# A smaller ring for GpSimd's dynamic DMAs and a seventh gate/up weight buffer in its place

## The reference, cut to what matters

```python
x = x + m @ w_out
f = hier_moe(rmsnorm(x, ln2_g).reshape(B * T, D), w_rg, b_rg, w_re, b_re, wg, wu, wd)
return x + f.reshape(B, T, D)
...
for g in range(N_GROUPS):
    hg = jnp.einsum('td,edf->tef', x, wg[g])
    hu = jnp.einsum('td,edf->tef', x, wu[g])
    hh = jax.nn.silu(hg) * hu * comb[:, g, :, None]
    y = y + jnp.einsum('tef,efd->td', hh, wd[g])
```

## Time and profile before

| what | value |
|---|---|
| median of 3 runs | 772.43 us |
| lowest, highest | 770.75, 772.51 us |
| the profiled execution: span from first to last instruction | 779.7 us |
| PE busy | 716.8 us (92%) |
| DVE, ACT, POOL busy | 397.7, 212.9, 194.6 us |
| HBM read, written | 154.27, 25.78 MB |
| mean granted TensorE clock | 0.952 |

### The profile page before, as it was taken

One profiled execution on the slowest core, in us unless ns is written; L12 is line 12 of the kernel. 1 busy time (PEld: TensorE's weight loads), 2 busy tenths in 40 slices (PEclk: granted clock), 3 DMA queues, 4 the chain that ended last, 5 costly groups with the idle time before them and its releaser, 6 DMA issues.

```text
span 779.7 us, 11121 instructions
## 1 busy us (share of the span) xinstructions
PE 716.8 (92%) x4071; PEld 349.9 (45%) x4071; DVE 397.7 (51%) x1107; ACT 212.9 (27%) x502; POOL 194.6 (25%) x208
## 2 busy tenths in 40 slices
PE   9999999899999999999999769999999999789293
PEld 6555556566666655455555532233232332222040
DVE  0776677754875854765655732333223332211275
ACT  3565646412452463112211201011110111000032
POOL 1011111010230333111112136544455444300111
PEclk9999999999999999899999869999999999779787
DMA  8911030030110016772221968699999999999794
GB/s 317 339 55 42 28 124 1 28 142 1 61 61 0 1 54 253 256 282 106 84 109 66 387 224 306 235 357 358 345 413 425 422 427 424 424 427 424 309 388 198
DMA packets 35544, 173.56 MB, mean 223 GB/s; under 512 B 6882, under 2 KB 13486, under 8 KB 25226
## 3 DMA queue, kind: packets, MB, share of 16 engines
q1 hardware_dynamic: 27058, 154.27, 50.5%
q0 software_dynamic: 8000, 17.24, 5.9%
q10 hardware_dynamic: 432, 1.34, 0.4%
HBM read 154.27 MB, written 25.78 MB: 231 GB/s over the span
## 4 chain that ended last, share of the span: by engine, by line
PE 65%; DVE 13%; DMA 9%; ACT 5%; issue 5%; SPq 1%; POOL 1%; DVEq 0%; POOLq 0%; ACTq 0%
PE PS L2185 17%; PE PS L2201 9%; PE PS L2004 6%; PE PS L1996 6%; PE PS L1982 4%; PE PS L1832 4%; DMA BIG<-in_wexp 4%; PE PS L1963 3%; PE PS L1833 2%; PE PS L1952 2%; DVE RD L1220 2%; DMA RD<-xtab,rot 2%; DMA BIG<-ypair 2%; PE PS L1816 2%; PE PS L2044 1%
## 5 line engine op out<-in xcount | busy, mean ns | idle before, releaser
L2185 PE MATMUL PS<-BIG,RD 128*32 128x512 f32 x1408 | 166.7, 620 | 13.3 <-issue 10.3
L2185 PEld LDWEIGHTS PS<-BIG,RD 128*32 128x32 f32 x1408 | 46.0, 114 | 118.3 <-issue 118.3
L876 POOL DMA_INDIRECT RD<-xtab,rot x84 | 85.0, 1012 | 35.5 <-issue 24.4
L2201 PE MATMUL PS<-BIG,RD 128*32 128x512 f32 x616 | 79.7, 592 | 2.0 <-DMA BIG<-in_wexp 0.9
L1684 DVE SCALAR_TENSOR_TENSOR RD<-RD,PS 128x256 f32<-128x256 f32 x22 | 9.2, 418 | 141.7 <-ACT RD L1140 141.7
L1832 PE MATMUL PS<-BIG 128*128 128x512 f32 x128 | 66.1, 598 | 0.3 <-DMA BIG<-in_wqkv 0.3
L773 POOL TENSOR_TENSOR stat<-stat,mhalf 128x1 f32<-128x1 f32 (+1 forms) x27 | 15.5, 575 | 188.9 <-DVE stat L1210 84.0
L1140 ACT ACTIVATE RD<-PS 128x256 f32<-128x256 f32 x22 | 8.4, 383 | 192.5 <-PE PS L2185 145.3
L2004 PE MATMUL PS<-BIG 128*128 128x512 f32 x128 | 60.5, 617 | 0.0
L1996 PE MATMUL PS<-BIG 128*128 128x512 f32 x128 | 59.2, 607 | 0.0
L1982 PE MATMUL PS<-BIG 128*128 128x344 f32 x192 | 57.3, 454 | 0.0
(11 more groups left out here) (321 smaller groups left out, 1017.9 us busy)
## 6 DMA issues: line engine op xcount, KB each, us to landing
BIG<-in_wexp SPq DMA_DIRECT2D x30, 2048.0 KB
BIG<-in_wexp SPq DMA_DIRECT2D x32, 1024.0 KB, 36.8
BIG<-ypair SPq DMA_DIRECT2D x8, 1024.0 KB, 9.9
xin<-in_x SPq DMA_DIRECT2D x13, 512.0 KB
BIG<-in_wxy SPq DMA_DIRECT2D x4, 1024.0 KB, 4.7
xin<-in_wexp SPq DMA_DIRECT2D x4, 1024.0 KB
BIG<-x2d SPq DMA_DIRECT2D x1, 4096.0 KB
out_y<-RD SPq DMA_DIRECT2D x8, 512.0 KB, 3.4
```

What stands on the lines that cost most here:

```text
L876: pool.indirect_dma_start(xg[:, p3, j * CHUNK_D:(j + 1) * CHUNK_D], None, xtab.rearrange("t (q e) -> (t q) e", q=NQ), bass.IndirectOffsetO ...
L2185: o = MM(PS[own, 2 + p2, :], xgT[:, p2, at:at + STRIP], wgu[place_of(n, j) % NG][:, k * 512:(k + 1) * 512], start=(k == 0), stop=(k == KD ...
L2201: o = MM(PS[own, 5 + half, :], hT[:, p2, k, own], wdn[place_of(n, j) % ND][:, at:at + 512], start=(k == 0), stop=(k == KF - 1))
```

## The change

The ring for the DMAs that GpSimd issues gets 4096 bytes a partition instead of the default. The room goes to `RD`, now 12288 words a partition. There are seven gate/up buffers. Buffer 3 lies at the end of `RD`, so its first load need not wait for the output projection and is issued with those of places 0 and 1. The second half of the projection's weights, which was buffer 3, becomes buffer 6; its first load is place 6, issued when the order is known. The final gain moves over the attention masks in `cst`. `F_G` stays 2, and the x2d load waits for the last users of buffers 5 and of down buffer 6, written with their numbers.

```diff
@@ -66,8 +66,9 @@
-NG = 6
+NG = 7
 ND = 7
+RING = 4096
@@ -75,7 +76,7 @@
-F_G, F_D = (NE - NG) % NG, (NE - ND) % ND
+F_G, F_D = 2, (NE - ND) % ND
@@ -209,8 +210,10 @@
         wgu = [big[:, i * GUW:(i + 1) * GUW] for i in range(2)]
-        wgu += [big[:, n_e + i * GUW:n_e + (i + 1) * GUW] for i in range(2)]
+        rd = sb("RD", [P, 3 * GUW])
+        wgu += [big[:, n_e:n_e + GUW], rd[:, 2 * GUW:3 * GUW]]
         wgu += [big[:, n_a + D_MODEL + i * GUW:n_a + D_MODEL + (i + 1) * GUW] for i in range(2)]
+        wgu += [big[:, n_e + GUW:n_e + 2 * GUW]]
@@ -227,7 +230,7 @@
-        RD = Region(sb("RD", [P, 9240])[:, :])
+        RD = Region(rd[:, :])
@@ -296,9 +299,9 @@
-        RD.phase(RD.words - D_MODEL)
-        gfb = RD.cut(D_MODEL)
-        blank = gfb[:, D_MODEL - 2 * NCOL:].bitcast(I32).rearrange("p (n c) -> p n c", c=2)
+        gfb = cst[:, K_MASK:K_MASK + D_MODEL]
+        RD.phase(RD.words - 2 * NCOL)
+        blank = RD.cut(2 * NCOL).bitcast(I32).rearrange("p (n c) -> p n c", c=2)
@@ -475,8 +478,8 @@
-        gu_in = [sem("gu_in%d" % i) for i in range(4)] + x_in
-        GU_IN = [0, 0, 0, 0, 80, 64]
+        gu_in = [sem("gu_in%d" % i) for i in range(4)] + x_in + [vnew_in]
+        GU_IN = [0, 0, 0, 0, 80, 64, 16]
@@ -644,6 +647,7 @@
             load_gu(0)
             load_gu(1)
             load_dn(0)
+            load_gu(3)
@@ -665,7 +669,6 @@
             sp.wait_ge(op_ps, 2 * NT)
-            load_gu(3)
             load_dn(3)
             load_dn(4)
@@ -681,7 +684,8 @@
             def load_gu_at(p, r):
                 e = ordered(p)
-                sp.wait_ge(gu_ps, r + 1)
+                if r >= 0:
+                    sp.wait_ge(gu_ps, r + 1)
@@ -700,7 +704,8 @@
             sp.wait_ge(ord_ok, 1 + ORD_OK)
-            load_dn_at(NG, -1)
+            load_gu_at(NG - 1, -1)
+            load_dn_at(ND - 1, -1)
@@ -722,8 +727,8 @@
-            sp.wait_ge(gu_ps, last_round(NE - NG + 3) + 1)
-            sp.wait_ge(y_ps, 2 * last_round(NE - ND + 2) + 2)
+            sp.wait_ge(gu_ps, last_round(NE - 6) + 1)
+            sp.wait_ge(y_ps, 2 * last_round(NE - 5) + 2)
@@ -2375,7 +2380,7 @@
-    nc = bacc.Bacc("TRN2", target_bir_lowering=False, num_devices=1)
+    nc = bacc.Bacc("TRN2", target_bir_lowering=False, num_devices=1, dynamic_dma_scratch_size=RING)
```

## The result

| | before | after |
|---|---|---|
| median | 772.47 us (770.75 to 774.43, 4 runs) | 762.53 us (761.19 to 763.70, 4 runs) |
| profiled execution: time, span | -, 779.7 us | 761.19, 759.4 us |
| PE busy | 716.8 us | 705.4 us |
| mean granted TensorE clock | 0.952 | 0.962 |

The medians are 9.9 us apart. The ratio is 0.9879, 95% interval 0.9854 to 0.9905, which is 9.3 us (7.3 to 11.3).

What follows compares the result with a forecast made beforehand. The landing of the last expert weight byte was taken to set the end, with 19 us of TensorE slack. Bytes -4.95 us plus gathers +1.0 gave -3.95, from 772.43 to 768.5 us; range 764.8 to 773.5.

Steps and rivals of the forecast that it cites:

- (e): Smaller ring for POOL's DMAs: strip gathers never wait for room, up to 0.7 us more a DMA would be hidden; cost 0.
- Rival D: Gathers lose nothing and an earlier round 0 spares another microsecond: 766.5 us, chance 0.12.
- (c): Place 6 loaded at about 456.5 us takes 2.10 MB from the full stretch after 570 us: last weight lands 4.95 us earlier.
- E: The change moves nothing, since the load queue runs empty somewhere in the tail and takes the bytes there: 772.4 us, chance 0.03.
- (a): Place 3's gate/up load moved from 437 to 304 us: next x load 4.95 us later, hidden by TensorE's projection; cost 0.
- (b): Place 3's load gone from the queue at 437 us: first gather and round 0 start 2 us earlier; gain on path 0.
- (d): Strip gathers for rounds 1 and 2 meet the extra load: 0 to 1.9 us more together, 1.0 taken; each at most 7.3.
- A: Gathers eat the gain: gather 1 late by the whole 4.95 us, gather 2 up to 1.2 more; 772.4 to 773.6 us, chance 0.15.
- C: Ring too small, so POOL waits for each DMA to land: some 440 us more in all, chance 0.02.
- The 7.3 us between profile and median: Profiled span 779.7 us against median 772.43: one slow matmul stretch, a round of 18.1 us instead of 10.8, could be the difference.
- B: Full DMA engines at 464 to 469 us cause a second slow-issue stretch in round 0 or 1: 7.3 us, 775.8 us, chance 0.08.

Runs made afterwards that it cites:

- one and two doses: Kernel before, half the gate/up columns of two places (one dose) or four (two doses) not loaded: 766.06 us (ratio 0.9937) and 762.26 us (0.9870).

## Why the prediction was wrong, point by point

- **The step that failed is (e), the ring.** It asked only whether a smaller ring costs something during the rounds, answered 0, and put no gain into the sum or the range. GpSimd's closing DRAIN measures 9.44 us with the default ring and 2.17 with 4096 bytes, and 5.0 us of that were on the path. The profile of before showed it: the span was 779.7 us, and the chain that ended last came to its last instruction about 772.4 us. Of the 7.3 us between them, 2.1 are the landing of the last output and 5.0 GpSimd's DRAIN; the prediction did not ask about them. Rival D, more than forecast, had another cause and 2 us of it, and its 766.5 us were still 4 us too high.
- **(c) right.** -4.95 us forecast, -5.2 to -5.4 in the traces, 4.9 and 10.0 us by the runs with one and two doses. Share and rate in the full stretch stayed at 1.01 and 424 GB/s, so E fell.
- **(a) and (b) right.** Counted from the x2d store ahead of it, the x load moved from 10.7 to 15.9 us, 5.2 where 4.95 was forecast, and its reader waited for TensorE as before. With the load gone from 437 us round 0 starts 1.1 us earlier on average, counted from the first issue of gather 1, where (b) said 2, and the early load alone moved the time by no more than the runs scatter.
- **(d): the size nearly right, one part missing.** 1.0 us was taken, 0 to 1.9 allowed; the traces give 1.2 from the first issue of gather 1, or 2.3 from the start of round 0, which is itself earlier. Gather 1 took 8.67 us where I held 7.3 for the most. And there was a second part that the step did not have, the clock; that the mean still lies near 1.0 is luck. The chain, and busy time by stretch, kernel after:

```profile
455.17 8.67 DMA RD<-xtab,rot
...
466.02 5.34 PE PS L2190 x32
...
471.72 3.62 PE PS L2190 x32
```

```profile
464.00:466.00 2.00, 0.04 (x4) 0.01 (x1) 2.00 (x2) 0.38 (x1) 1.02 (x2) 1.00 0.79 201
466.00:468.00 2.00, 1.98 (x12) 0.72 (x16) 0.60 (x2) 0.00 (x0) 1.70 (x2) 0.57 0.85 344
```

  TensorE stood idle for 2 us while gather 1 was late, and then the granted clock fell from 1.00 to 0.57: mostly its lower level, 1.2 GHz. 32 gate/up matmuls take 5.34 us there and the next 32 take 3.62 at full clock. Three of the five traces of the changed kernel have this, after 1.98, 1.99 and 2.33 us of idle time. In the two others TensorE stood 1.64 and 1.85 us and the clock stayed. None of the ten with six buffers falls back in rounds 0 to 2, and neither do the two with the load behind both gathers. From the start of round 0 to that of round 2 the three take 24.4 to 24.7 us, the two 22.4 and 23.1.
- **A and C wrong, as weighed.** Gather 1 took 2.1 us more and not 4.95, gather 2 of two other kernels landed under full engines, and POOL's 84 gathers still take 1.01 us:

```profile
L881 POOL DMA_INDIRECT RD<-xtab,rot x84: 1001/1009/1049, 451.2 to 659.5; - x84
```

- **The 7.3 us between profile and median: the stretch fits.** See the last section. But there were two gaps of 7.3 us, this one and that between the end of the chain and the end of the span, and I explained only the first. B did not come: no new slow stretch in round 0 or 1.

## What to carry to other kernels

Compare the end of the chain that ended last with the end of the span, and look at the closing DRAIN of each engine: GpSimd's costs 0.6 us here for each KB of the dynamic-DMA ring between 4 and 8 KB, and it is free only where GpSimd ends that much before the last output has landed. So let GpSimd's last work end early, or make the ring as small as its DMAs allow. Bytes taken out of a full stretch are worth their time at the full rate, but the place they are moved to has a price: a gather beside them, and a clock that can fall when TensorE waits for it.

## What the runs showed that was not expected

**Round 2 is slow in some sets of runs and not in others, whatever the kernel.** In the four sets at 780 us all 13 traces have the stretch of the earlier trace rows; in the set at 772.17 us none of the four has it, nor has the trace of after behind the result above. It makes round 2 longer by 6.3 to 9.1 us (17.1 to 19.9 us instead of 10.8; 15.8 us with the second load of place 6), which is about what the two levels of the kernel before differ by. The changed kernel has traces at both levels: from the start of round 0 to the last down matmul 256.0 and 258.1 us at the lower, 265.3 to 267.3 at the higher. The kernel before has no trace at the lower one. The trace that stands before the prediction has the stretch, with a span of 779.7 us; that the runs beside it, at 772.4, had none is argued from their time. As each set ran on its own chip, whether chip or occasion decides it is open. The chain of the changed kernel in a set with it, and in the set without:

```profile
485.76 1.31 PE PS L2190 x4
...
487.19 1.31 PE PS L2190 x4
...
488.62 1.07 PE PS L2190 x4
```

```profile
483.25 7.00 PE PS L2190 x64
```

TensorE issues some four matmuls each 1.43 us there. What makes it do so is open. Rival B supposed that such a stretch needs full DMA engines. In the first of these traces they are full only at its start; from 490 to 496 us, still within it, their share is 0.02 to 0.25. Instructions that arrive late are one guess. The next 16 KB packet of the profile's instruction queue moves 2.6 us before to 1.3 us after the end of the stretch in ten of the thirteen traces; in the first of these two it moves between 496 and 497 us, and the stretch ends at 495.7. But in two others the stretch ends 5.0 us before that packet moves, and with the second load of place 6 it begins only as the packet moves. So a wait for this packet does not account for all of them; and no run tried it. The Trainium skill, page "Runtime: NRT & Kernel Launch", section "Instruction fetch mechanics", calls the cost of crossing such a 16 KiB block mostly hidden; no run here shows whether the 6.3 to 9.1 us are that cost.

**GpSimd's DRAIN hardly depends on when its DMAs ran.** With the default ring it took 9.12 us right after the last scatter had landed (734.3 us, roots left out), and 9.44 us in the kernel before, when that was 34 us back (from 735.9 to 770.1 us).
